# Dilated-window attention on one Trainium2 core: heads taken in pairs on halves of the TensorE array, groups combined in the same stage

## The chip, the core and the metric

The kernel runs on 1 core of one Trainium2 chip. The metric is the device time of one execution in microseconds (us). PE is TensorE (PEld its weight loads), DVE is VectorE, ACT is ScalarE, POOL is GpSimd and SP is the queue that issues every DMA here.

## The reference, cut to what matters

A sequence of 1024 prompt tokens and one of 256 sample tokens (1280 rows, 10 tiles of 128) go through an attention layer, a state-space layer and a last norm, all in float32. Only the attention layer is touched. It has three groups of 16 heads of 64 dims, with dilations 1, 4 and 16 and windows 128, 512 and 2048:

```python
proj = hn @ w_in                       # q, k, v of each group, and one gate z of 1024 columns
for g, (window, dilation) in enumerate(GROUP_PATTERNS):
    q = _rope(qkv[:, :, g, 0]); k = _rope(qkv[:, :, g, 1]); v = qkv[:, :, g, 2]
    o, lse = _dilated_window_attention(q, k, v, dilation, window // (2 * dilation))
wts = softmax(stack(lses), axis=0)     # per token and head, over the three groups
o = einsum('gbsh,gbshd->bshd', wts, stack(outs))
y = o.reshape(b, s, 1024) * silu(z)
return y @ w_out
```

## The kernel before, in words

Stages follow one another, each in its own block: `norm_stage`, `attend_stage`, `combine_stage`, `out_stage` ("mix"), two state-space stages ("front", "back"), "glu" and `out_stage` again ("final").

**Attend.** A unit is a pair of heads of one group, 24 units in all, group by group. `steps()` gives 25 rows: a row projects unit n while unit n-1 attends. A projection is three weight tiles (K, Q, V), each of three chunks of 512, 512 and 256 tokens, each chunk 8 k-tiles by 3 split products (`project`, L848; hi and lo parts in fp32r). A row has 22 slots; each slot gives PE one score (L794), one transpose step (L803), one value step (L816) of one head of one tile, and then 10 projection matmuls. The score of a head contracts 64 dims, so it uses 64 of PE's 128 rows: weights are 128 queries, up to 256 keys stream past. The key windows are 128, 192 or 256 wide (`windows`); the sample tiles of groups 1 and 2 use all 256 sample keys and a mask of residues. DVE adds the mask and takes the minimum (L721), ACT takes the exponential with its row sum (L642), PE transposes the probabilities, DVE copies them out (L731), and in the value step the transposed probabilities (128 keys by 128 queries) are the weights and 64 columns of values stream past, so the output is tokens by dims; ACT copies it out (L649) and SP stores it by token into `o_scratch`. The buffers `sc`, `sm`, `pr`, `tr`, `pt` have two halves, used by alternate steps.

Rope: SP swaps halves of K or Q by DMA (`sw`), POOL multiplies by the sine (L618), DVE by the cosine (L740) and adds (L752). At the start of a row the unit's V is transposed through `pj` (L828), and ACT copies it out before the next projection may use `pj`. POOL also computes 16 "powers" tasks for the state-space layer (64 or 65 steps, one task per row in rows 1 to 16), and stores each in DRAM.

**Combine.** The stage loads the gate weights, projects z (480 matmuls of 512 columns), loads the three groups' outputs and statistics, computes the group shares once for all heads, weighs and adds the three outputs, multiplies by silu(z), transposes y (80 transposes) and stores it to `y_scratch`. Beside that it loads the eight "f" results of POOL's tasks, transposes them (128 transposes) and stores them.

Every engine runs its instructions in the order written; waits are on semaphores.

Of the kernel before, what the change touches and what calls it, by code (L numbers as in the profile page):

```python
# [21 lines left out]
F32R = mybir.dt.float32r  # L22
# [4 lines left out]
P = 128  # L27
# [36 lines left out]
POWER_TASKS = 2 * NB  # L64
POWER_END = [L * 2 * (t + 1) + L * 6 * (t + 1) + max(t + 1 - NB, 0) for t in range(POWER_TASKS)]

MASKS = {"at0": (0, 256), "at64": (256, 256), "at128": (512, 256), "class64": (768, 128),
         "mod4": (896, 256), "mod16": (1152, 256)}  # L70
MASK_COLS = 1408


def mask_table(np):

    q = np.arange(P)[:, None]
    k = np.arange(256)[None, :]
    ok = [np.abs(k - q) <= HALF, np.abs(k - 64 - q) <= HALF, np.abs(k - 128 - q) <= HALF,
          (k[:, :128] // 64) == (q // 64), (k - q) % 4 == 0, (k - q) % 16 == 0]
    return np.where(np.concatenate(ok, axis=1), 0.0, -BIG).astype(np.float32)  # L80


def windows(g):
# [15 lines left out]
    first = len(value_blocks(g)) - 2  # L99
    for i in range(2):  # L100
        mask = ("at0", "at128")[i] if g == 0 else ("mod4" if g == 1 else "mod16")
        out.append((PROMPT, 256, mask, [(first, 128, 0), (first + 1, 128, 128)]))
# [284 lines left out]
ATT_STEPS = 2 * TILES  # L387
SLOTS = ATT_STEPS + 2
UNIT_MMS = 3 * len(CHUNKS) * KT
PER_SLOT = -(-3 * UNIT_MMS // SLOTS)  # L390
CHUNK_MMS = 3 * KT
K_TILE, Q_TILE, V_TILE = range(3)


def chunk_slot(c):

    return (CHUNK_MMS * (c + 1) - 1) // PER_SLOT


def attend_stage(nc, w_att, tables, masks_d, ident_d, hT, o_scratch, st_scratch, a, ab_d, decay_d,  # L400
                 seeds, placed_d):
    with ExitStack() as ctx:
        m = Mem(nc, ctx, "att")
        raw = m.sb("raw", [P, 2, KT, P])
        wh = m.sb("wh", [P, 3, KT, P], F32R)
        wl = m.sb("wl", [P, 3, KT, P], F32R)
# [4 lines left out]
        val = m.sb("val", [P, 2, 11, P])  # L411
# [4 lines left out]
        pt = m.sb("pt", [P, 2, 256])  # L416
        o_sb = m.sb("o", [P, TILES, P])
# [4 lines left out]
        place = m.sb("place", [P, 2, GB, L, SC])  # L422

# [4 lines left out]
        st = m.sb("stats", [P, TILES, HEADS, 2])  # L428
        pj = m.ps("pj", [P, 3, 512])
        sc = m.ps("sc", [P, 2, 512])  # L430
        tr = m.ps("tr", [P, 2, 512])
        po = m.ps("po", [P, 512])

# [8 lines left out]
        o_stored, seed_in, pool_step, place_stored = (  # L442
            m.sem(n) for n in ("o_stored", "seed_in", "pool_step", "place_stored"))
        st_stored = m.sem("st_stored")
# [3 lines left out]


        def steps():  # L450
            for n in range(UNITS + 1):
                yield (n - 1 if n >= 1 else None), (n if n < UNITS else None)

        def to_class_order(dst, src, g, lo, n):

            d = DILATION[g]
            if g == 0 or lo >= PROMPT:
                return dst[:, lo:lo + n], src[:, 0:n]
            a, b = lo // d, (lo + n) // d
            return (dst[:, 0:PROMPT].rearrange("p (r l) -> p r l", r=d)[:, :, a:b],  # L460
                    src[:, 0:n].rearrange("p (l r) -> p r l", r=d))

        @block.sync
        def _(sp):
            def raw_load(n):
                if n >= 2:
                    sp.wait_ge(w_hi, n - 1)
                    sp.wait_ge(w_lo, n - 1)
                sp.dma_start(raw[:, n % 2], w_att[n // 3, n % 3]).then_inc(raw_in[n % 2], 16)

            def swap(unit, which):
                n = 2 * unit + which
                sp.wait_ge(chunk_out, 9 * unit + 3 * (which + 1))
                if n >= 1:
                    sp.wait_ge(rope_done, n)
                for a in range(4):
                    b = a ^ 1
                    sp.dma_start(sw[32 * a:32 * a + 32, :], t[32 * b:32 * b + 32, which, :]).then_inc(swapped, 16)

            def by_class(sb, dram, g, done):  # L480

                if g == 1:
                    v = dram[0:PROMPT].rearrange("(a p r) c -> a p r c", a=2, r=4)
                    for a in range(2):
                        sp.dma_start(v[a], sb[:, a:PT:2, :]).then_inc(done, 16)
                elif g == 2:
                    v = dram[0:PROMPT].rearrange("(l i b) c -> b l i c", i=PT, b=2)
                    for b in range(2):
                        sp.dma_start(v[b], sb[64 * b:64 * b + 64, 0:PT, :]).then_inc(done, 16)
                else:  # L490
                    v = dram[0:PROMPT].rearrange("(h i p) c -> h p i c", h=2, p=P)
                    for h in range(2):
                        sp.dma_start(v[h], sb[:, 4 * h:4 * h + 4, :]).then_inc(done, 16)
                v = dram[PROMPT:TOK].rearrange("(i p) c -> p i c", p=P)
                sp.dma_start(v, sb[:, PT:TILES, :]).then_inc(done, 16)

            def load_seed(task):
                kind, b = divmod(task, NB)
                if task >= 1:
                    sp.wait_ge(pool_step, POWER_END[task - 1])  # L500
                    kind1, b1 = divmod(task - 1, NB)
                    sp.dma_start(seeds[kind1][:, :, b1 * GB:(b1 + 1) * GB], seed[:]).then_inc(place_stored, 16)
                    sp.dma_start(placed_d[kind1][b1], place[:].rearrange("p r g t c -> p r g (t c)"))\
                      .then_inc(place_stored, 16)
                if 1 <= task < POWER_TASKS:
                    sp.wait_ge(place_stored, 32 * task)
                if task < POWER_TASKS:
                    sp.dma_start(seed[:], a[("b", "c")[kind]][:, :, b * GB:(b + 1) * GB]).then_inc(seed_in, 16)

            def store(unit):  # L510
                g, pair = divmod(unit, PAIRS)
                sp.wait_ge(o_out, TILES * (unit + 1))
                by_class(o_sb[:], o_scratch[g][:, pair * P:(pair + 1) * P], g, o_stored)
                if pair == PAIRS - 1:
                    sp.wait_ge(expd, ATT_STEPS * (unit + 1))
                    by_class(st[:].rearrange("p i h s -> p i (h s)"), st_scratch[g], g, st_stored)
# [6 lines left out]
            raw_load(2)  # L523
            for j, name in ((4, "a_re"), (5, "a_im"), (6, "log_step")):
                sp.dma_start(params[:, j], a[name]).then_inc(param_in, 16)
            for att, proj in steps():
                if proj is not None and proj + 1 < UNITS:
                    raw_load(3 * (proj + 1) + K_TILE)
                if proj is None:
                    break  # L530
                if proj + 1 < UNITS:
                    raw_load(3 * (proj + 1) + Q_TILE)
                swap(proj, K_TILE)
                if proj + 1 < UNITS:
                    raw_load(3 * (proj + 1) + V_TILE)
# [7 lines left out]
                if 1 <= proj <= POWER_TASKS + 1:  # L543
                    load_seed(proj - 1)
# [1305 lines left out]
```

## Time and profile before

| | |
|---|---|
| runs | 2867.34, 2868.78, 2869.9 us (median 2868.78) |
| span of the profiled execution | 2864.4 us; its own time is not recorded, the span is 4.4 us below the median |
| PE / DVE / ACT / POOL busy over the span | 2581.1 / 1287.2 / 848.1 / 797.2 us |
| attend stage, from its first projection (us 53) | to us 1769 |
| combine stage | to us 1931 |
| later stages | us 1931 to 2864 |
| DMA | 298.43 MB, 33.4% of 16 engines' span |

Times in a profile are counted from the start of the span. A float32 matmul stands in the trace as two MATMUL records. A matmul's recorded duration includes its pipeline, so what it costs PE is read from the start of one record to the start of the next, not from the duration.

### The profile page before, as it was taken

The page shows a single profiled execution, that of the slowest core. Times are in us where ns is not written, and L with a number is a line of the kernel's source. Part 1 is how long each engine was busy: PE and PEld are TensorE (multiplying, and loading weights), DVE is VectorE, ACT ScalarE, POOL GpSimd, SP SyncE. Part 2 cuts the span into 40 slices and gives each one's busy share as a digit, 9 for nine tenths or more (in the row PEclk, how much of TensorE's full clock was granted, in tenths as well). Part 3 has the DMA queues.
Part 4 walks back from the last instruction along what each step waited for, and adds up shares of the span by engine and source line. Part 5 has one row for each costly group of instructions (what it writes and reads, how often), then busy time and mean ns, then how long its engine had stood idle before and what let it go on. Part 6 is the DMA issues. An engine that isn't in the chain of part 4 may idle for free. (4 is left out here: it accounts for less than half of the span.)

```text
span 2864.4 us, 39052 instructions
## 1 busy us (share of the span) xinstructions
PE 2581.1 (90%) x13832; PEld 2035.0 (71%) x13832; DVE 1287.2 (45%) x2871; ACT 848.1 (30%) x2178; POOL 797.2 (28%) x1303
## 2 busy tenths in 40 slices
PE   5999999999999999999999998898889993267978
PEld 4777777777777777777777776777678873265767
DVE  5333333334444444443344434754322799725434
ACT  4233233332223222223333333323244320014222
POOL 1644444444444444443101110211011110121200
PEclk9999999999999999999999996999999997588989
DMA  4122222222222222222212112876465450384333
GB/s 149 50 58 69 69 69 69 66 64 69 69 69 69 69 62 69 69 62 74 59 50 60 52 41 72 301 254 208 158 206 162 143 151 20 90 239 165 133 138 125
DMA packets 173481, 298.43 MB, mean 104 GB/s; under 512 B 32880, under 2 KB 107632, under 8 KB 170096
## 3 DMA queue, kind: packets, MB, share of 16 engines
q1 hardware_dynamic: 173296, 296.00, 33.4%
q8 instruction: 112, 1.84, 0.3%
q14 instruction: 73, 0.60, 0.1%
HBM read 177.80 MB, written 86.67 MB: 92 GB/s over the span
## 5 line engine op out<-in xcount | busy, mean ns | idle before, releaser
L848 PE MATMUL att_pj<-hT_hi,att_wh 128*128 128x512 f32 (+1 forms) x1728 | 633.7, 367 | 20.7 <-ACT att_val L674 10.6
L848 PE MATMUL att_pj<-hT_lo,att_wh 128*128 128x512 f32 (+1 forms) x1728 | 631.4, 365 | 0.0
L848 PE MATMUL att_pj<-hT_hi,att_wl 128*128 128x512 f32 (+1 forms) x1728 | 630.5, 365 | 0.0
L721 DVE CUSTOM_DVE_ANT_0 att_sm<-att_sc,att_mask 128x256 f32<-128x256 f32 (+2 forms) x480 | 179.9, 375 | 930.5 <-PE att_sc L794 915.6
L642 ACT ACTIVATE att_pr<-att_sm,att_stats 128x256 f32<-128x256 f32 (+2 forms) x480 | 225.7, 470 | 927.1 <-DVE att_stats L721 926.5
L618 POOL TENSOR_TENSOR att_sw<-att_sw,att_rope 128x1280 f32<-128x1280 f32 x48 | 146.2, 3045 | 913.8 <-DMA att_sw<-att_t 913.7
L848 PEld LDWEIGHTS att_pj<-hT_hi,att_wh 128*128 128x128 f32 x1728 | 328.1, 190 | 68.7 <-issue 17.6
L848 PEld LDWEIGHTS att_pj<-hT_hi,att_wl 128*128 128x128 f32 x1728 | 328.0, 190 | 43.6
L848 PEld LDWEIGHTS att_pj<-hT_lo,att_wh 128*128 128x128 f32 x1728 | 328.7, 190 | 41.5
L794 PE MATMUL att_sc<-att_qk 64*128 64x256 f32 (+2 forms) x960 | 302.9, 396 | 4.5 <-DVE att_qk L752 4.5
L816 PE MATMUL att_po<-att_val,att_pt 128*128 128x64 f32 (+1 forms) x1664 | 257.8, 266 | 0.0
L816 PEld LDWEIGHTS att_po<-att_val,att_pt 128*128 128x128 f32 (+1 forms) x1664 | 241.9, 198 | 9.5 <-issue 3.0
L794 PEld LDWEIGHTS att_sc<-att_qk 64*128 64x128 f32 x960 | 144.5, 189 | 141.1 <-issue 115.3
L803 PE MATMUL att_tr<-att_ident,att_pr 128*128 128x128 f32 (+1 forms) x832 | 197.7, 307 | 0.3 <-ACT att_pr L642 0.2
L803 PEld LDWEIGHTS att_tr<-att_ident,att_pr 128*128 128x128 f32 (+1 forms) x832 | 87.9, 138 | 120.4 <-issue 106.1
L667 ACT COPY att_t<-att_pj 128x512 f32<-128x512 f32 (+1 forms) x216 | 111.4, 516 | 200.0 <-PE att_pj L848 196.7
L731 DVE COPY att_pt<-att_tr 128x256 f32<-128x256 f32 (+1 forms) x384 | 145.7, 379 | 41.3 <-PE att_tr L803 39.8
L597 POOL TENSOR_TENSOR att_prod<-att_power,att_ab 128x128 f32<-128x128 f32 x416 | 158.0, 412 | 8.4
L158 PE MATMUL front_pj<-front_hh,front_wh 128*128 128x512 f32 (+1 forms) x384 | 139.9, 364 | 15.6 <-DVE front_hl L1445 15.6
L740 DVE TENSOR_TENSOR att_t<-att_t,att_rope 128x1280 f32<-128x1280 f32 x48 | 144.3, 3007 | 19.9 <-DMA att_sw<-att_t 19.8
L160 PE MATMUL front_pj<-front_hh,front_wl 128*128 128x512 f32 (+1 forms) x384 | 137.0, 357 | 0.0
L159 PE MATMUL front_pj<-front_hl,front_wh 128*128 128x512 f32 (+1 forms) x384 | 136.8, 356 | 0.0
(234 smaller groups left out, 3959.0 us busy)
## 6 DMA issues: line engine op xcount, KB each, us to landing
att_raw<-in_w_att_dram SPq DMA_DIRECT2D x72, 512.0 KB, 3.6
att_sw<-att_t SPq DMA_DIRECT2D x192, 160.0 KB, 2.8
comb_o<-o_scratch SPq DMA_DIRECT2D x60, 256.0 KB, 4.3
o_scratch<-att_o SPq DMA_DIRECT2D x48, 256.0 KB, 3.1
placed_f<-att_place SPq DMA_DIRECT2D x8, 1024.0 KB, 4.5
e_scratch<-att_place SPq DMA_DIRECT2D x8, 1024.0 KB, 4.5
comb_fpre<-placed_f SPq DMA_DIRECT2D x16, 512.0 KB, 5.5
f_scratch<-comb_ft SPq DMA_DIRECT2D x16, 512.0 KB, 4.0
```

The costliest lines, as they stand in the source:

```text
L158: pe.matmul(out, lh, rh, start=first, stop=False)
L160: return pe.matmul(out, ll, rh, start=False, stop=last)
L597: pool.tensor_tensor(prod[:, j], old[:, x], y, ALU.mult).then_inc(pool_step, 1)
L618: pool.tensor_tensor(sw[:], sw[:], rope[:, 1], ALU.mult).then_inc(sin_done, 1)
L642: act.activation(pr[:, n % 2, 0:w], sm[:, n % 2, 0:w], ACT.Exp, bias=st[:, s // 2, h, 0:1], scale=-1.0, accum_out=st[:, s // 2, h, 1:2]).t ...
L721: dve.tensor_tensor_reduce(sm[:, n % 2, 0:w], sc[:, n % 2, 0:w], mask[:, a:a + w], -SCALE, 3e38, ALU.add, ALU.min, st[:, s // 2, h, 0:1]). ...
L731: last = dve.tensor_copy(pt[:, n % 2, 0:P * len(pieces)], tr[:, n % 2, 0:P * len(pieces)])
L740: dve.tensor_tensor(t[:, which], t[:, which], rope[:, 0], ALU.mult).then_inc(cos_done, 1)
L794: pe.matmul(sc[:, n % 2, 0:w], qk[rows, unit % 2, Q_TILE, i * P:(i + 1) * P], qk[rows, unit % 2, K_TILE, k0:k0 + w], start=True, stop=True ...
L803: last = pe.transpose(tr[0:k, n % 2, j * P:(j + 1) * P], pr[:, n % 2, c0:c0 + k], ident[:])
L816: last = pe.matmul(po[:, h * HD:(h + 1) * HD], pt[0:k, n % 2, j * P:(j + 1) * P], val[0:k, unit % 2, b, h * HD:(h + 1) * HD], start=(j == ...
L848: last = pe.matmul(pj[:, c % 3, 0:n], w[:, which, kt], h[:, kt, lo:lo + n], start=(r == 0), stop=(r == CHUNK_MMS - 1))
```

## The change

`combine_stage` is gone. `attend_stage` now has units ordered pair by pair (the three groups of a pair one after another), 26 rows of 12 slots, and a fourth weight tile (Z) in every third unit. A slot handles one tile for both heads: two scores on rows 0 to 63 and 64 to 127 of PE into two banks, value steps whose weights are the values (64 columns for head 0, 64 for head 1) and whose moving operand is the transposed probabilities, so the output is dims by tokens with head 0 on partitions 0 to 63 and head 1 on 64 to 127, and then the transposes. Between slots come 18 projection matmuls (24 in rows with four weight tiles). Sample tiles of groups 1 and 2 are put into class order too, so that their windows are 128 wide. `sm`, `pr`, `pt`, `sc`, `tr` now have one half per head, and `val` one copy. The outputs stay on chip, in four buffers of 128 by 1280; ACT scatters classes back to tokens while copying. Per unit the statistics go to DRAM by token (SP: 1, 4 or 10 DMAs) and come back per pair (3 DMAs). In each row n = 4, 7, ... 25 DVE and ACT compute the shares of one pair, and in nine steps ACT spreads a share over 64 dims, PE transposes it into the bank `aux`, and DVE multiplies, adds and gates (18 instructions of up to 512 columns); SP stores y of the pair. The V transposes use `aux` as well, in three parts with projection matmuls between. POOL's 16 tasks lie in rows 2 to 17; the eight "f" results are transposed by PE in slots 3 to 6 of the row after (`f_turn`), copied by ACT and stored by SP, in place of the way over DRAM.

```diff
-        first = len(value_blocks(g)) - 2
-            mask = ("at0", "at128")[i] if g == 0 else ("mod4" if g == 1 else "mod16")
-            out.append((PROMPT, 256, mask, [(first, 128, 0), (first + 1, 128, 128)]))
+        if g == 0:
...
+        else:
+            out.append((P * i, 128, ("class64", "class16")[g - 1], [(i, 128, 0)]))
...
-SLOTS = ATT_STEPS + 2
-PER_SLOT = -(-3 * UNIT_MMS // SLOTS)
+SLOTS = STEPS + 2
+def per_slot(unit):
+    return 3 * w_count(unit) * CHUNK_MMS // SLOTS
...
             for n, att, proj, comb in rows():
                 if proj is not None:
                     raw_load(base + 2)
...
+                if n in TURN_ROW:
+                    f_store(TURN_ROW[n], 0)
+                if proj is not None:
+                    raw_load(base + 3)
+                    swap(proj, K_TILE)
...
+                    stats_store(att)
+                    if att % GROUPS == GROUPS - 1:
+                        stats_load(att // GROUPS)
...
+            def combine(pair, k):
...
+                dve.wait_ge(bcast_done, 9 * pair + k + 1)
+                dve.tensor_tensor(own, own, aux[:, 0:n], ALU.mult).then_inc(comb_step, 1)
+                if g >= 1:
+                    dve.wait_ge(comb_step, at + 1)
+                    dve.tensor_tensor(own, own, before, ALU.add).then_inc(comb_step, 1)
+                if g == 2:
+                    dve.wait_ge(comb_step, at + 2)
+                    dve.tensor_tensor(own, own, gate[:, cols], ALU.mult).then_inc(comb_step, 1)
...
             def score(unit, s):
-                n = ATT_STEPS * unit + s
-                if n >= 2:
-                    pe.wait_ge(masked, n - 1)
-                rows = slice(64 * h, 64 * h + 64)
-                pe.matmul(sc[:, n % 2, 0:w], qk[rows, unit % 2, Q_TILE, i * P:(i + 1) * P],
-                          qk[rows, unit % 2, K_TILE, k0:k0 + w], start=True, stop=True).then_inc(scored, 1)
+                n = STEPS * unit + s
+                if n >= 1:
+                    pe.wait_ge(masked, 2 * n)
+                for h in range(2):
+                    head = slice(64 * h, 64 * h + 64)
+                    pe.matmul(sc[:, h, 0:w], qk[head, unit % 2, Q_TILE, s * P:(s + 1) * P],
+                              qk[head, unit % 2, K_TILE, k0:k0 + w], start=True, stop=True).then_inc(scored, 1)
...
             def values(unit, s):
...
                 for j, (b, k, _) in enumerate(pieces):
-                    last = pe.matmul(po[:, h * HD:(h + 1) * HD], pt[0:k, n % 2, j * P:(j + 1) * P],
-                                     val[0:k, unit % 2, b, h * HD:(h + 1) * HD],
-                                     start=(j == 0), stop=(j == len(pieces) - 1))
+                    for h in range(2):
+                        head = slice(64 * h, 64 * h + 64)
+                        last = pe.matmul(po[head, 0:P], val[0:k, b, head], pt[0:k, h, j],
+                                         start=(j == 0), stop=(j == len(pieces) - 1))
...
+            def f_turn(task, q, att):
+                if q == 0:
+                    pe.wait_ge(pool_step, POWER_END[task])
+                    pe.wait_ge(vturn_out, 3 * (att + 1))
...
+                for j in range(4):
+                    last = pe.transpose(aux[:, j * P:(j + 1) * P],
+                                        place[:, j % 2, 2 * q + j // 2].rearrange("p t c -> p (t c)"), ident[:])
...
                     if att is not None and s < STEPS:
                         score(att, s)
+                    if att is not None and s >= 2:
+                        values(att, s - 2)
+                    if att is not None and 1 <= s <= STEPS:
                         turn(att, s - 1)
...
+                    if n in TURN_ROW and 3 <= s < 7:
+                        f_turn(TURN_ROW[n], s - 3, att)
+                    if comb is not None and s >= 3:
+                        broadcast(comb, s - 3, att)
...
-def combine_stage(nc, w_z, ident_d, hT, o_scratch, st_scratch, y_scratch, placed_f, f_scratch):
```

## Rows read from the trace of the kernel before

**Rows 1.** Stretches: us, busy PE PEld DVE ACT POOL (records), PEclk, DMA share, GB/s.

```profile
103.00:1737.00 1634.00, 1619.34 (x8553) 1229.79 (x8553) 649.38 (x1670) 496.91 (x1509) 622.30 (x1150) 1.00 0.22 63
1737.00:1769.00 32.00, 31.68 (x120) 23.29 (x118) 12.48 (x58) 13.16 (x52) 0.00 (x0) 0.58 0.09 21
1769.00:1931.00 162.00, 138.60 (x689) 115.91 (x688) 99.17 (x132) 49.66 (x91) 29.97 (x20) 0.92 0.81 268
```

**Rows 2.** PE in order of time, 256-wide step: start us, us, line, matmul, count.

```profile
634.97 0.28 PE L848 MATMUL att_pj<-hT_hi,att_wh 128*128 128x256 f32 x1
635.08 0.28 PE L848 MATMUL att_pj<-hT_lo,att_wh 128*128 128x256 f32 x1
635.29 0.70 PE L794 MATMUL att_sc<-att_qk 64*128 64x256 f32 x2
635.92 0.44 PE L803 MATMUL att_tr<-att_ident,att_pr 128*128 128x128 f32 x2
636.20 0.56 PE L816 MATMUL att_po<-att_val,att_pt 128*128 128x64 f32 x4
636.56 0.36 PE L848 MATMUL att_pj<-hT_hi,att_wl 128*128 128x256 f32 x1
636.76 0.28 PE L848 MATMUL att_pj<-hT_hi,att_wh 128*128 128x256 f32 x1
```

**Rows 3.** The same of a 128-wide step, with two 512-column projections ahead.

```profile
1384.66 0.40 PE L848 MATMUL att_pj<-hT_hi,att_wl 128*128 128x512 f32 x1
1384.89 0.40 PE L848 MATMUL att_pj<-hT_hi,att_wh 128*128 128x512 f32 x1
1385.22 0.48 PE L794 MATMUL att_sc<-att_qk 64*128 64x128 f32 x2
1385.63 0.33 PE L803 MATMUL att_tr<-att_ident,att_pr 128*128 128x128 f32 x1
1385.80 0.33 PE L816 MATMUL att_po<-att_val,att_pt 128*128 128x64 f32 x2
1385.94 0.47 PE L848 MATMUL att_pj<-hT_lo,att_wh 128*128 128x512 f32 x1
1386.25 0.39 PE L848 MATMUL att_pj<-hT_hi,att_wl 128*128 128x512 f32 x1
```

**Rows 4.** PE in the front stage: matmuls on rows 0-63 (L1509) and 64-127 (L1513).

```profile
2252.03 0.27 PE L1509 MATMUL front_states_ps<-front_f,front_ub 64*16 64x112 f32 x1
2252.04 0.27 PE L1513 MATMUL front_states_ps<-front_f,front_ub 64*16 64x112 f32 x1
2252.13 0.26 PE L1509 MATMUL front_states_ps<-front_f,front_ub 64*16 64x112 f32 x1
```

**Rows 5.** POOL in order of time: the Q sine, and the end of the task after it.

```profile
825.77 2.91 POOL L618 TENSOR_TENSOR att_sw<-att_sw,att_rope 128x1280 f32<-128x1280 f32 x1 [21.48 <-DMA att_sw<-att_t]
...
862.61 0.85 POOL L570 COPY att_place<-att_power 64x256 f32<-64x256 f32 x2
```

**Rows 6.** Groups by line and form, us 103 to 1737: busy us, mean ns, idle before.

```profile
L740 DVE TENSOR_TENSOR att_t<-att_t,att_rope 128x1280 f32<-128x1280 f32 x46 | 141.4, 3073 | 0.6 <-DMA att_sw<-att_t 0.5
L721 DVE CUSTOM_DVE_ANT_0 att_sm<-att_sc,att_mask 128x256 f32<-128x256 f32 x252 | 106.5, 422 | 417.0 <-PE att_sc L794 416.4
L642 ACT ACTIVATE att_pr<-att_sm,att_stats 128x256 f32<-128x256 f32 x252 | 128.4, 510 | 533.7 <-DVE att_stats L721 533.4
```

**Rows 7.** The last row, PE in order of time, two scores one step apart.

```profile
1754.65 0.79 PE L794 MATMUL att_sc<-att_qk 64*128 64x128 f32 x2
...
1756.11 0.79 PE L794 MATMUL att_sc<-att_qk 64*128 64x128 f32 x2
```

**Rows 8.** A DVE group of the combine stage, us 1769 to 1931.

```profile
L1028 DVE TENSOR_TENSOR comb_o<-comb_o 128x512 f32<-128x512 f32 x20 | 13.8, 692 | 0.7
```

**Rows 9.** DMA issues of one line on SP: ns min/median/max, first and last start.

```profile
L495 SPq DMA_DIRECT2D st_scratch<-att_stats x3: 556/624/639, 691.4 to 1773.7; - x3
```

**Rows 10.** DMA issues: count, KB each, median us from issue to landing.

```profile
comb_stats<-st_scratch SPq DMA_DIRECT2D x3, 160.0 KB, 4.3
```

More of the change, by code:

```diff
@@ L510, in store @@
[L510 to L516, printed above, removed]
+                for x in range(4):
+                    y = x ^ 1
+                    sp.dma_start(sw[32 * x:32 * x + 32, :], t[32 * y:32 * y + 32, which, :]).then_inc(swapped, 16)
@@ new lines, in f_evac, with share_exp @@
+            def f_evac(task, q):
+                b = POWERS[task][2]
+                act.wait_ge(f_turned, 4 * b + q + 1)
+                if 4 * b + q:
+                    act.wait_ge(f_stored, 16 * (4 * b + q))
+                if q == 0 and POWERS[task][0] >= 4:
+                    act.wait_ge(bcast_done, 9 * ((POWERS[task][0] - 1) // GROUPS))
+                act.copy(ft[:], aux[:].rearrange("p (g r n) -> p g r n", g=2, r=2)).then_inc(f_out, 1)
+            def share_exp(pair):
+                act.wait_ge(shares, SHARE_STEPS * pair + 3)
+                act.activation(ex[:], gap[:], ACT.Exp).then_inc(exps, 1)
@@ new lines, in share_spread @@
+            def share_spread(pair, k):
+                g, c = divmod(k, 3)
+                lo, n = CHUNKS[c]
+                i, tiles = lo // P, n // P
+                if k == 0:
+                    act.wait_ge(shares, SHARE_STEPS * (pair + 1))
+                    act.wait_ge(f_stored, 16 * 4 * sum(1 for row in TURN_ROW if row < GROUPS * pair + 4))
+                else:
+                    act.wait_ge(bcast_done, 9 * pair + k)
+                act.copy(wide[:, 0:2 * tiles].rearrange("p (i h) d -> p i h d", h=2),
+                         share[:, i:i + tiles, g].unsqueeze(3).to_broadcast([P, tiles, 2, HD])).then_inc(spread, 1)
@@ L742, in rotate @@
             def rotate(unit, which):
-                n, g = 2 * unit + which, unit // PAIRS
+                n, g = 2 * unit + which, unit % GROUPS
                 dve.wait_ge(cos_done, n + 1)
@@ new lines, in value_turn @@
+            def value_turn(unit, b):
+                blocks = value_blocks(unit % GROUPS)
+                if unit + b:
+                    pe.wait_ge(vturn_out, 3 * unit + b)
+                if b == 0:
+                    pe.wait_ge(const_in, 48)
+                    pe.wait_ge(chunk_out, 3 * (w_base(unit) + 3))
+                    turns = sum(1 for row in TURN_ROW if row <= unit)
+                    if turns:
+                        pe.wait_ge(f_out, 4 * turns)
+                    if unit >= 4:
+                        pe.wait_ge(comb_step, COMB_STEPS * ((unit - 1) // GROUPS))
+                for j in range(4 * b, min(4 * b + 4, len(blocks))):
+                    k0, k = blocks[j]
+                    last = pe.transpose(aux[0:k, (j - 4 * b) * P:(j - 4 * b + 1) * P], t[:, 0, k0:k0 + k], ident[:])
+                last.then_inc(vturn_done, 1)
@@ new lines, in broadcast @@
+            def broadcast(pair, k, att):
+                g, c = divmod(k, 3)
+                lo, n = CHUNKS[c]
+                pe.wait_ge(spread, 9 * pair + k + 1)
+                if k == 0:
+                    pe.wait_ge(vturn_out, 3 * (UNITS if att is None else att + 1))
+                else:
+                    pe.wait_ge(comb_step, COMB_STEPS * pair + comb_steps(k - 1) + 1)
+                for j in range(n // P):
+                    last = pe.transpose(aux[:, j * P:(j + 1) * P],
+                                        wide[:, 2 * j:2 * j + 2].rearrange("p h d -> p (h d)"), ident[:])
+                last.then_inc(bcast_done, 1)
```

791 lines of the change are left out of this document (358 added, 433 removed).

## The prediction

> **What bounds the kernel now.** I cut the span into stretches first. From us 103 to 1737, the 23 rows in which one unit projects while another attends, PE is busy 1619 of 1634 us at the full clock of 2.4 GHz, while DVE has 649, ACT 497 and POOL 622 [rows 1]. So a row lasts as long as PE's own list, 71.0 us each, and only work taken from that list, or a new wait in it, changes the time. Then come 32 us for the last unit, with nothing to project and a granted clock of 0.58, mostly the lower level of 1.2 GHz, and 162 us of combine, in which PE is busy 139 us, mostly with z [rows 1].
>
> Second I read PE in order of time around one step, from start to start. A 512-column projection record takes 0.23 us (1384.66 to 1384.89), a 256-column one about 0.12 (636.76 less its 0.08 of delay, below). The 256-wide step of one head takes: 0.09 from the end of the projection (635.08 + 0.12) to the score, 0.63 for the score's two records, 0.28 for two transposes, 0.36 for the values' four records, 0.08 by which the second projection behind it is late: 1.44 us [rows 2]. The 128-wide step takes 0.10, 0.41, 0.17, 0.14 and 0.08: 0.90 us [rows 3]. The differences give unit prices. 128 more columns in each of two score records cost 0.22 us, so 0.11 us per 128 columns and record. One transpose costs 0.11 (0.28 less 0.17), with 0.06 fixed. Two value records cost 0.22, 0.11 each, though only 64 columns stream, half of what 0.11 us carries: there the 128-column weight load sets the pace. Of a 128-wide score's 0.41, 0.22 stream; 0.19 are a first weight load (0.11) and the change of array shape (0.08). Third, the front stage has two chains of float32 matmuls on rows 0 to 63 and 64 to 127: 112 columns in steps of 0.10 us (2252.03 to 2252.13), the other half 0.01 behind [rows 4]. Halves by rows run side by side.
>
> **The change, part by part.** *Scores.* Both heads side by side cost one head's score plus 0.11 for the second half's weights: 0.74 for 256 keys, 0.52 for 128. *Values.* The weights are now 64 columns (0.055, an estimate: half the load above), 128 columns stream (0.11 a record), two records per head and piece. No row shows halves by columns. Bounds: wholly side by side, 0.11 x 4 for a wide tile; one after the other, 0.11 x 8. I take side by side, since the nearest row, the halves by rows, is [rows 4]. With two first loads (0.11) and a change of shape (0.09) that is 0.64, narrow 0.42. *Transposes* stay 0.11 each: 0.06 + 0.44, narrow 0.06 + 0.22. A wide tile of both heads so costs 0.09 + 0.74 + 0.64 + 0.50 + 0.08 = 2.05 in place of 2.88; a narrow one 1.40 in place of 1.80; a sample tile of groups 1 and 2, wide before and narrow now, 1.40 in place of 2.88.
>
> The Trainium skill, "TensorEngine Tiling (Array Packing)", Key Properties, has tiles of columns, too, load and multiply in parallel; by that the sum stays as it is, and no run here shows it yet.
>
> In the 23 rows stand 8 units each of groups 0 and 1 and 7 of group 2: 80 + 64 wide tiles (0.83 saved), 30 sample tiles (1.48), 56 narrow ones (0.40): 119.5 + 44.4 + 22.4 = 186 us off PE. Two smaller ends of the list I take by estimate: the tiles with a 64-key piece change shape once more per head before and once per pair now (48 tiles, some 0.4 us each from the 0.09 and 0.11 above: 19 us), and PE no longer waits for the V copies before it projects (some 0.4 us a row, an ACT copy: 10 us). The rows then take 1634 - 186 - 29 = 1419 us.
>
> *Added to PE.* z moves in with the same columns, 480 x 0.23 = 110 us. The f transposes: 128 x 0.11 + 32 x 0.1 = 17. The shares: 30 transposes and nine changes a pair, 30 x 0.11 + 9 x 0.15 = 4.7, seven pairs: 33. Rows 1 to 23: 1579 us. A single row: projection 144 x 0.23 + 72 x 0.12 = 42 us (56 with a Z tile), its ten tiles 20.5, 19.2 or 14.0 for groups 0, 1, 2, V and the rest 1 to 2, shares 4.7 in rows that attend group 0: about 69, 78 and 58 us.
>
> *Covered work.* DVE gains 18 instructions a pair at 0.69 [rows 8] or less, some 11 us; with its 28 us a row (649 over 23) and statistics it holds some 45 us in a row of 69. ACT and DVE per tile: two masks at 0.42 and two exponentials at 0.51, each with a short read of its sum [rows 6]: 2.5 us in line, while the transposes wait for the exponentials only one slot later. Slots are 4.8 to 6.5 us long (those rows by 12). The cosine, 3.07 us [rows 6], stands ahead of the next mask on DVE; two such slots per row can shift a mask by a microsecond or three, inside that slack. `o_scratch` and the f detour were DMA beside PE in the rows (DMA share 0.22 [rows 1]): nothing. The per-unit statistics are 1, 4 or 10 issues at 0.62 us [rows 9] on SP behind the row's loads; the shares read them a slot and a half into the next row, some 15 us on: nothing, and if that cover is gone, DVE and ACT stop in slot 1 and PE at the score of slot 3. SP's f stores stand ahead of the K load and swap; they delay a swap by some 3 us in four rows, and the rotation has more than a slot.
>
> *The new wait.* `f_turn` puts PE behind POOL. From a Q sine's start to its task's end POOL takes 37.7 us (825.77 to 863.46) [rows 5]. In a 69 us row the sine starts at about 8 slots + 4.5 us = 50.5, the task ends at 88, `f_turn` comes at 69 + 3 x 6.5 + 1.5 = 90: 2 us to spare, four times; 9 us the other four times. Behind `f_turn` are queued the slot's 18 or 24 projections and the next score. I put 10 us for all waits, 0 to 40 as bounds.
>
> *The end.* Before, 194 us follow the last full row [rows 1]. Now: ten slots of the last unit at the low clock (a step of one head takes 1.46 there [rows 7], a pair some 2.2): 24 with the V transposes; then in line ten issues of statistics at 0.62 and their landing (2.3, an estimate at half of the 4.3 of a load [rows 10]), three loads and 4.3 [rows 9, 10]: 14.7; shares 3; nine steps of transposes, multiply, add, gate at 0.69 [rows 8]: 16; the store of y 3.5. 61 us, bounds 50 to 75.
>
> **Sum.** 1579 + 10 + 61 = 1650 in place of 1634 + 194 = 1828: 178 us less. The span of 2864.4 becomes 2686; the median lies 4.4 us above the span, so 2691, rounded to **2690 us**. 0.2% (6 us) is about what a measurement of this kernel tells from no change.
>
> **Rivals.**
> *Columns in turn.* The two column halves stream one after the other: 144 x 0.44 + 86 x 0.22 = 82 us more: 2772. For it: no row shows the contrary; against it: halves by rows. Chance 0.13.
> *Loads in turn, too.* Every value record waits for its own 64-column load, as both halves share the same rows: 8 x 0.055 a wide tile and 4 x 0.055 a narrow one more, 82 us again: 2854. Against it: the old value records, all on the same rows, start 0.11 apart [rows 2, 3], the time of the load alone; load and stream in turn would be 0.165. Chance 0.03. The Trainium skill, "TensorE: Matmul & The Clock Gate", Part 3, says that a weight load overlaps matmuls in flight only when the row group differs; by that this rival would be the time, and the trace disagrees.
> *POOL holds PE: slower.* Place: `f_turn` in slot 3 of eight rows. A busier DVE or a late swap lengthens the task; each us past the 2 (or 9) to spare is a us of PE. It decides from some 28 us of added length in each of eight tasks (178 / 8 = 22, and the slack of 5 or 6): with tasks longer by 31 us, about twice theirs, 2690 + 4 x 29 + 4 x 22 = 2894. Against it: POOL took the same steps beside a DVE at 40% [rows 1, 5]. Chance 0.04.
> *No overlap at all.* Rows and columns both in turn (scores dearer by 0.32 and 0.11: 56 us): 2690 + 82 + 56 = 2828. Against it stand rows 4. Chance 0.02.
>
> **Numbers.** The forecast has 0.78. Its own range: 32 us lower if the second loads (0.14 a tile, 230 tiles) hide as well, 10 without waits, 11 with a short end: 2637; 30 us higher with the waits at their bound: 2720, and 14 for the end. Taking in the first rival with some waits, 2635 to 2785. Faster 0.95, within 0.2% 0.01, slower 0.04.
>
> **What would show it.** Right: attention rows of about 69, 78 and 58 us with PE over 97% busy; in one slot score to values 0.74 and to the transposes 0.64 more; value records of head 1 beginning within 0.06 of head 0's. Wrong: value records all 0.11 or 0.16 apart in one line; PE idle at `f_turn` with POOL as releaser; DVE or ACT waiting for the statistics; an end much longer than 61 us.

## The result, and the profile after

The changed kernel takes **2628.35 us** (median of 4 runs, 2625.17 to 2635.17) in place of 2868.34 (2867.34 to 2869.9, 4 runs): a ratio of 0.9168, 95% interval 0.9154 to 0.9181. The forecast was 2690, its range 2635 to 2785: the time lies 62 us under the forecast and 7 under the low end. The profiled execution took 2628.88 us, its span is 2627.0.

The same cut into stretches as [rows 1]: rows 1 to 23, then the end of the attend stage (last unit, last shares, store of y), then mix and all behind it.

```profile
101.00:1632.00 1531.00, 1507.71 (x9287) 1187.43 (x9287) 639.82 (x1583) 578.71 (x1667) 693.55 (x1141) 1.00 0.24 64
1632.00:1697.00 65.00, 30.39 (x135) 16.83 (x133) 21.41 (x76) 21.59 (x66) 0.00 (x0) 0.52 0.08 12
1697.00:2627.00 930.00, 722.99 (x4176) 608.29 (x4176) 477.72 (x909) 249.39 (x459) 115.53 (x77) 0.89 0.47 150
```

PE still sets the rows: busy 1508 of 1531 us, at a granted clock that rounds to 1.00 (three short stretches at the lower level stand below). By the starts of the V transposes, rows 1 to 23 last from 100.9 to 1631.6, 1530.7 us, where 1589 was forecast (1579 and 10 of waits). The end lasts to 1697.4: 65.8 us, forecast 61, bounds 50 to 75. So the miss lies in the rows, 58 us.

One wide tile of both heads, PE in order of time, beside [rows 2]:

```profile
1200.15 0.39 PE L1066 MATMUL att_pj<-hT_hi,att_wl 128*128 128x512 f32 x1
1200.47 0.70 PE L982 MATMUL att_sc<-att_qk 64*128 64x256 f32 x4
1201.10 0.66 PE L1005 MATMUL att_po<-att_pt,att_val 128*64 128x128 f32 x8
1201.69 0.66 PE L992 MATMUL att_tr<-att_ident,att_pr 128*128 128x128 f32 x4
1202.10 0.36 PE L1066 MATMUL att_pj<-hT_hi,att_wh 128*128 128x256 f32 x1
1202.30 0.28 PE L1066 MATMUL att_pj<-hT_lo,att_wh 128*128 128x256 f32 x1
...
1258.18 0.28 PE L1066 MATMUL att_pj<-hT_hi,att_wl 128*128 128x256 f32 x1
1258.39 0.49 PE L982 MATMUL att_sc<-att_qk 64*128 64x128 f32 x4
1258.81 0.44 PE L1005 MATMUL att_po<-att_pt,att_val 128*64 128x128 f32 x4
1259.18 0.44 PE L992 MATMUL att_tr<-att_ident,att_pr 128*128 128x128 f32 x2
1259.37 0.36 PE L1066 MATMUL att_pj<-hT_hi,att_wh 128*128 128x256 f32 x1
1259.57 0.28 PE L1066 MATMUL att_pj<-hT_lo,att_wh 128*128 128x256 f32 x1
```

Read from start to start. The four score records of both heads take 0.63 us to the values, exactly what the two records of one head took in [rows 2]. Eight value records take 0.59, though eight in line would stream for 0.88. Four transposes take 0.41. With 0.09 ahead (1200.15 + 0.23 to 1200.47) and 0.08 behind (1202.30 - 1202.10, less 0.12) the tile costs 1.80 us; the forecast was 2.05. The narrow tile, below it, costs 0.09 + 0.42 + 0.37 + 0.19 + 0.08 = 1.15 in place of 1.40.

PE's waits within the rows (releaser: us in total, times, longest):

```profile
PE att_aux L1024 <- ACT att_val L782: 12.4, 15, 1.1
PE att_aux L1035 <- POOL att_place L653: 9.5, 4, 2.6
```

L1024 are the V transposes, L1035 the f transposes: the "new wait" of the prediction is there, four times. Of the 12.4 us at V, 12.1 fall in the seven rows that attend group 2.

### The profile page after: what moved, and what is told of

Same layout as the page of the kernel before. It is cut to its first block and busy times, and to the rows that moved or that the text cites. A ratio compares the mean times of both kernels' runs of the same rounds, so it can differ in the third digit from the quotient of the medians.

```text
span 2627.0 us, 38336 instructions
## 1 busy us (share of the span) xinstructions
PE 2325.1 (89%) x13896; PEld 1865.8 (71%) x13896; DVE 1185.6 (45%) x2668; ACT 886.2 (34%) x2256; POOL 841.2 (32%) x1283
## 5 line engine op out<-in xcount | busy, mean ns | idle before, releaser
L1066 PE MATMUL att_pj<-hT_hi,att_wh 128*128 128x512 f32 (+1 forms) x1920 | 710.0, 370 | 10.8 <-DVE att_wl L848 10.8
L860 DVE CUSTOM_DVE_ANT_0 att_sm<-att_sc,att_mask 128x128 f32<-128x128 f32 (+2 forms) x480 | 152.4, 355 | 561.6 <-PE att_sc L982 560.4
L730 ACT ACTIVATE att_pr<-att_sm,att_stats 128x128 f32<-128x128 f32 (+2 forms) x480 | 215.0, 449 | 434.1 <-PE att_tr L992 313.0
L879 DVE TENSOR_TENSOR att_t<-att_t,att_rope 128x1280 f32<-128x1280 f32 x48 | 71.8, 1495 | 201.8 <-DMA att_sw<-att_t 201.8
L870 DVE COPY att_pt<-att_tr 128x512 f32<-128x512 f32 (+1 forms) x192 | 107.0, 557 | 110.2 <-PE att_tr L992 110.0
L1005 PE MATMUL att_po<-att_pt,att_val 128*64 128x128 f32 (+1 forms) x1536 | 146.5, 295 | 6.4 <-ACT att_o L751 5.9
L982 PE MATMUL att_sc<-att_qk 64*128 64x128 f32 (+2 forms) x960 | 146.0, 382 | 0.0
L992 PE MATMUL att_tr<-att_ident,att_pr 128*128 128x128 f32 (+1 forms) x768 | 138.8, 294 | 0.0
L1005 PEld LDWEIGHTS att_po<-att_pt,att_val 128*64 128x64 f32 (+1 forms) x1536 | 79.0, 136 | 72.8 <-issue 52.9
L891 DVE TENSOR_TENSOR att_qk<-att_t,att_sw 128x1024 f32<-128x1024 f32 (+1 forms) x80 | 107.9, 1383 | 48.4 <-issue 34.9
```

The lines of the kernel that those rows point to most:

```text
L730: act.activation(pr[:, h, 0:w], sm[:, h, 0:w], ACT.Exp, bias=st[:, unit % 2, s, h, 0:1], scale=-1.0, accum_out=st[:, unit % 2, s, h, 1:2]) ...
L860: dve.tensor_tensor_reduce(sm[:, h, 0:w], sc[:, h, 0:w], mask[:, x:x + w], -SCALE, 3e38, ALU.add, ALU.min, st[:, unit % 2, s, h, 0:1]).the ...
L982: pe.matmul(sc[:, h, 0:w], qk[head, unit % 2, Q_TILE, s * P:(s + 1) * P], qk[head, unit % 2, K_TILE, k0:k0 + w], start=True, stop=True).th ...
L992: last = pe.transpose(tr[0:k, h, j], pr[:, h, c0:c0 + k], ident[:])
L1005: last = pe.matmul(po[head, 0:P], val[0:k, b, head], pt[0:k, h, j], start=(j == 0), stop=(j == len(pieces) - 1))
L1066: last = pe.matmul(pj[:, c % 3, 0:n], w[:, k % 2, kt], h[:, kt, lo:lo + n], start=(r == 0), stop=(r == CHUNK_MMS - 1))
```

## Experiments on the halves

The theory after this reading: the second half, of rows or of columns, costs PE nothing at all, neither its stream nor its weight load. Rival 1 is the prediction's own price (the second load is paid, 0.11 us for scores and 0.055 for values), with the 58 us coming from elsewhere; rival 2 is halves in turn.

**One head's scores left out.**

```diff
-                for h in range(2):
-                    head = slice(64 * h, 64 * h + 64)
-                    pe.matmul(sc[:, h, 0:w], qk[head, ...], qk[head, ...]).then_inc(scored, 1)
+                pe.matmul(sc[:, 0, 0:w], qk[0:64, ...], qk[0:64, ...]).then_inc(scored, 2)
```

> Left out: the score of head 1 (its mask step reads head 0's scores instead), so PE issues half of the score matmuls. Theory (the row half of head 1 loads its weights and streams wholly beside head 0): nothing is saved, 2628 us within 5. Rival 1 (the second half's weight load is paid in turn, 0.11 us a tile, as the prediction had it, and the 58 us by which rows 1 to 23 are shorter came from elsewhere): 240 tiles x 0.11 = 26 us less, 2602. Rival 2 (row halves stream in turn): 144 wide tiles x 0.44 + 96 narrow x 0.22 = 84 us less, 2544.

**One head's values left out.**

```diff
-                    for h in range(2):
-                        last = pe.matmul(po[head, 0:P], val[0:k, b, head], pt[0:k, h, j], ...)
+                    last = pe.matmul(po[0:64, 0:P], val[0:k, b, 0:64], pt[0:k, 0, j], ...)
```

> Left out: the value matmuls of head 1 (its half of the output stays zero), so PE issues half of the value matmuls. Theory (the column half of head 1 loads and streams wholly beside head 0): nothing is saved, 2628 us within 5. Rival 1 (second half's load paid in turn, 0.055 us a tile by the prediction's estimate): 240 x 0.055 = 13 us less, 2615. Rival 2 (column halves in turn): 144 x 0.44 + 96 x 0.22 = 84 us less, 2544.

**Both heads through the columns of one, and both through the rows of one.**

```diff
-                        last = pe.matmul(po[head, 0:P], val[0:k, b, head], pt[0:k, h, j], ...)
+                        last = pe.matmul(po[0:64, 0:P], val[0:k, b, head], pt[0:k, h, j], ...)
```

> Changed: head 1's values go through the column half of head 0 (both heads are added into partitions 0 to 63), the same number of matmuls with the same sizes. Theory (the change lives from two column halves working at once): each record of head 1 costs its 0.11 us of streaming, 144 x 4 x 0.11 + 96 x 2 x 0.11 = 84 us more, 2712; with its load of 0.055 in turn as well 126 us more, 2754. Rival 2 (column halves work in turn already): no difference, 2628 within 5.

```diff
-                    head = slice(64 * h, 64 * h + 64)
+                    head = slice(0, 64)
                     pe.matmul(sc[:, h, 0:w], qk[head, ...], qk[head, ...])
```

> Changed: head 1's score reads the queries and keys of head 0, on rows 0 to 63, the same number of matmuls with the same sizes. Theory (two row halves at once): 144 x 0.44 + 96 x 0.22 = 84 us more, 2712, and up to 26 us more where the second load of 0.11 us is not hidden: 2738. Rival 2 (row halves in turn already): no difference, 2628 within 5.

**Half of the transposes left out**, for a price to compare with.

```diff
-                for h in range(2):
-                    for j, (_, k, c0) in enumerate(pieces):
-                        last = pe.transpose(tr[0:k, h, j], pr[:, h, c0:c0 + k], ident[:])
+                for j, (_, k, c0) in enumerate(pieces):
+                    last = pe.transpose(tr[0:k, 0, j], pr[:, 0, c0:c0 + k], ident[:])
```

> Left out: the transposes of head 1's probabilities (head 0's are copied into both places), so PE issues half of the transposes. If each transpose costs 0.11 us of PE, as 16 f transposes cost 1.77 in a row of f_turn_later: rows that attend group 0 shorter by 2 x 10 x 0.11 = 2.1 to 2.2 us, group 1 by 2.0, group 2 by 1.1; in all 144 x 0.22 + 96 x 0.11 = 42 us, less some 8 that the four rows that wait for POOL keep: about 34 us less than the changed kernel, 2595. If transposes hide beside other work as the second halves do: rows the same and 2628 to 2631.

Medians: 2632.14 and 2630.15 us with half of the scores or of the values gone, 2690.05 and 2699.0 with both heads on one half of the rows or columns, 2599.41 with half of the transposes; the changed kernel itself, run again beside others, 2630.93. In rows without f transposes (from one row's first V transpose to the next; us):

| kernel | attends group 0, with shares | group 1, with a Z tile | group 2, with the waits at V |
|---|---|---|---|
| changed kernel | 64.53 | 73.57 | 57.07 |
| half the scores | 64.48 | 73.49 | 57.01 |
| half the values | 64.47 | 73.50 | 57.01 |
| scores on one row half | 68.52 | 76.96 | 59.00 |
| values on one column half | 68.88 | 77.42 | 59.22 |
| half the transposes | 62.39 | 71.69 | 55.95 |

Half of the matmuls of a step can go and a row of ten tiles gets 0.05 to 0.08 us shorter: rival 1 wanted 1.1 for the scores, 0.55 for the values. Put on one half, the same matmuls cost 0.40 us per wide score (64.53 to 68.52 in ten tiles) and 0.43 per wide value step: rival 2 falls by its own price. One wide tile of each, PE in order of time; first half the values, then values on one column half, then scores on one row half:

```profile
1184.56 0.70 PE L984 MATMUL att_sc<-att_qk 64*128 64x256 f32 x4
1185.19 0.65 PE L1007 MATMUL att_po<-att_pt,att_val 128*64 128x128 f32 x4
1185.77 0.66 PE L994 MATMUL att_tr<-att_ident,att_pr 128*128 128x128 f32 x4
```

```profile
1187.85 0.70 PE L984 MATMUL att_sc<-att_qk 64*128 64x256 f32 x4
1188.48 1.09 PE L1010 MATMUL att_po<-att_pt,att_val 128*64 128x128 f32 x8
1189.50 0.66 PE L994 MATMUL att_tr<-att_ident,att_pr 128*128 128x128 f32 x4
```

```profile
1181.57 1.13 PE L982 MATMUL att_sc<-att_qk 64*128 64x256 f32 x4
1182.63 0.66 PE L1005 MATMUL att_po<-att_pt,att_val 128*64 128x128 f32 x8
1183.21 0.66 PE L992 MATMUL att_tr<-att_ident,att_pr 128*128 128x128 f32 x4
```

Values take 0.58 us for four records on one half and 0.59 for eight on two; 1.02 for eight on one. Scores take 1.06 on one half and 0.63 on two. The transposes do cost: 2.14 us for twenty in a row of group 0, 0.11 each. Both kernels with heads on one half came out at 60 to 70 us more, not 84. Part of that is 0.40 and 0.43 in place of 0.44 a tile; the rest lies in the four rows of group 1 with f transposes. There the longer list took the place of the wait for POOL: PE waits for it 0.3 us once with values on one column half, and the profile lists no such wait with scores on one row half, so these rows stayed near the changed kernel's 77.9 to 79.8 (78.7 to 79.8 us). Half the transposes came out at 30 less, not 34: the same rows stayed at 78.7 to 80.2, since the four waits for POOL grew to 3.4 to 3.8 us each.

**The sample tiles.** Undone alone:

```diff
-            out.append((P * i, 128, ("class64", "class16")[g - 1], [(i, 128, 0)]))
+            out.append((PROMPT, 256, ("mod4", "mod16")[g - 1], [(PT, 128, 0), (PT + 1, 128, 128)]))
...
-ST_DMAS = (1, 4, 10)
+ST_DMAS = (1, 3, 3)
...
```

> Undone: the narrow sample tiles of groups 1 and 2 (their windows are all 256 sample keys again, with masks of residues; to make room the exponentials of the gaps are made in place). By the measured prices of a wide and a narrow tile (1.80 and 1.15) each such tile costs 0.65 more: rows that attend groups 1 and 2 longer by 1.3 us; rows 1 to 23: 30 x 0.65 = 20 less about 5 that the four rows waiting for POOL take up; the end: two tiles dearer by some 1 us and seven issues of statistics fewer, 7 x 0.63 = 4.4 us less. In all 10 to 13 us more than the changed kernel, 2640. Rival (the rows have slack there, or the scattered copies and ten issues cost as much as they save): within 4 us of it.

2657.13 us (2651.52 to 2659.64), 26 more than the changed kernel, where 10 to 13 were expected. Rows that attend groups 1 and 2 take 74.85 and 58.35, 1.28 more for two tiles: 0.64 a tile, as the two tiles above say (1.80 - 1.15), and 20 us over the rows. Two parts of the expectation fell. The four rows that wait for POOL took nothing up: the task they wait for begins in a row that attends group 0, which this edit leaves as it was. And the end stayed at 66 us with seven issues fewer: the last unit's V transposes and slots took 0.9 us more, as expected of two dearer tiles, and the statistics only 1.0 less. SP's DMA issues at the end, first of the changed kernel, then of this one:

```profile
1661.40 1.19 SPq L549 DMA_DIRECT2D st_scratch<-att_stats  x2
1662.63 5.07 SPq L554 DMA_DIRECT2D st_scratch<-att_stats  x8
1668.88 1.88 SPq L561 DMA_DIRECT2D att_pair_stats<-st_scratch  x3
```

```profile
1683.92 1.20 SPq L548 DMA_DIRECT2D st_scratch<-att_stats  x2
1685.16 1.48 SPq L549 DMA_DIRECT2D st_scratch<-att_stats  x1
1690.43 1.79 SPq L556 DMA_DIRECT2D att_pair_stats<-st_scratch  x3
```

From the first store to the load are 7.5 us with ten issues and 6.5 with three. SP waits 3.8 us behind the last of three issues and 1.2 behind the last of ten, since it is the one large store that is late: it holds both sample tiles and lands 5.3 us after its issue begins, while the last of the eight small pieces (an eighth of the sample rows each) lands 1.7 us after its own. The span of this profile is 21 us above that of the changed kernel run again (2649.7 and 2628.7), the median 26; the profiled execution was the fastest of the four, and the other 5 us stand in no profile.

## Experiments on the waits

**The f transposes one slot later**, with their copies; SP issues the stores behind the K swap.

```diff
-                    if n in TURN_ROW and 3 <= s < 7:
-                        f_turn(TURN_ROW[n], s - 3, att)
+                    if n in TURN_ROW and 4 <= s < 8:
+                        f_turn(TURN_ROW[n], s - 4, att)
```

> Edit: the f transposes, their copies and stores one slot later (slots 4 to 7). Theory (the 9.5 us that PE idles there in 4 pieces, with POOL as releaser, are the end of POOL's task, 2.3 to 2.6 us late against a slot of 6.5): 9.5 us less, about 2619, and no wait for POOL left. Rival (the stores then hold up the swap of Q or the next loads on SP, and the wait moves to the scores of the next row): no gain, 2628 or up to 10 us more.

**Silu one row later**, where no exponentials follow in the row.

```diff
-                        if s == SLOTS - 1 and w_count(proj) == 4:
-                            silu(proj)
+                    if att is not None and s == STEPS and w_count(att) == 4:
+                        silu(att)
...
                 act.activation(gate[:], gate[:], ACT.Silu).then_inc(gated, 1)
+                act.activation(warm[:], ident[0:1, 0:1], ACT.Exp)
```

> Edit: silu of the gate goes from the last slot of the row that projects z to slot 10 of the next row, where no exponentials are left, and a one-element exponential behind it brings the table of exponentials back there. Theory (the V transposes at the start of a row behind z wait for ACT, which then has two table loads of 1.28 us and a silu of 1.27 in hand): about 2.5 us less in each of 7 rows and 2 to 4 us less in the last row: 16 to 20 us less, about 2610. Rival (the waits of the V transposes, 16.4 us in 17 pieces, are those for ACT's copies alone, in any row): no more than 4 us less.

> The changed kernel as it is, beside the next three: 2628 us, rows 1 to 23 within 2 us of 1531.

> Both edits together. If they are independent: 25 to 30 us less than the changed kernel, 2598 to 2603; if both only fill the same slack of PE, no better than the better of the two.

Together on one chip: changed kernel 2630.93 us, f transposes later 2618.03, silu later 2623.78, both 2608.1 (again, on another occasion, 2610.54). The ratios to before are 0.9175 (0.9163 to 0.9188), 0.9125 (0.9113 to 0.9138), 0.9151 (0.9139 to 0.9164) and 0.9093 (0.9081 to 0.9106). The gains alone, 12.9 and 7.2 us, add up to 20.1, and both together gave 22.8: the edits are independent, though below the 25 to 30 expected, since silu gave too little. The rows of the changed kernel took 1527.7 us in this second profile, not within 2 of 1531; the reason is the clock, next.

The f transposes gave 12.9 us, more than the 9.5 of idle time, and no wait of PE for POOL is left. The rows that waited fell to 75.33 each: from 79.31, 79.79, 79.45 and 77.89 in the first profile of the changed kernel, 15.1 us, and from 79.47, 78.21, 77.89 and 77.89 in the second, 12.1 us. Why more than the idle time, PE in order of time shows in the first profile:

```profile
381.92 1.12 PE L1035 MATMUL att_aux<-att_ident,att_place 128*128 128x128 f32 x4 [2.30 <-POOL att_place L653]
382.69 0.78 PE L1066 MATMUL att_pj<-hT_hi,att_wh 128*128 128x512 f32 x1
383.27 0.63 PE L1066 MATMUL att_pj<-hT_lo,att_wh 128*128 128x512 f32 x1
383.69 0.63 PE L1066 MATMUL att_pj<-hT_hi,att_wl 128*128 128x512 f32 x1
384.12 0.63 PE L1066 MATMUL att_pj<-hT_hi,att_wh 128*128 128x512 f32 x1
384.55 0.59 PE L1066 MATMUL att_pj<-hT_lo,att_wh 128*128 128x512 f32 x1
384.97 0.40 PE L1066 MATMUL att_pj<-hT_hi,att_wl 128*128 128x512 f32 x1
385.21 0.40 PE L1066 MATMUL att_pj<-hT_hi,att_wh 128*128 128x512 f32 x1
```

Behind 2.30 us of idle the 512-column records start 0.43 us apart until 384.97 and 0.24 after: the lower level of the clock (1.2 GHz) until then, the higher (2.4 GHz) after. The granted clock over 4 us from the first f transpose on is 0.62 here, 0.69 and 0.57 behind the second and third wait, and 1.00 behind the fourth (us 990.57), also of 2.30 us, whose row is the one of 77.89. So with the same idle time the lower clock cost 1.4 us (79.31 less 77.89). In the second profile the same four waits are there, 2.3 to 2.6 us, but the clock fell behind the first alone (0.61, then 1.00 three times): that is why its rows are 3 us shorter.

Silu gave less than expected: 7.2 us in the medians. In the profiles each of the seven rows that attend group 2 is 0.8 us shorter (58.06 for 58.87, 56.28 for 57.07), 5.6 in all, and the end 5.1 (60.7); that profiled execution, 2618.69 us, was the fastest of five. ACT in order of time, end of a row of that kernel; ACT_TABLE_LOAD stands ahead of silu and, again, ahead of the exponential:

```profile
1482.27 0.59 ACT L773 COPY att_t<-att_pj 128x512 f32<-128x512 f32 x1 [2.71 <-PE att_pj L1069]
1482.87 1.28 ACT L777 ACT_TABLE_LOAD   x1
1484.16 1.27 ACT L777 ACTIVATE att_gate<-att_gate 128x1280 f32<-128x1280 f32 x1
1485.45 1.28 ACT L778 ACT_TABLE_LOAD   x1
1486.75 0.20 ACT L778 ACTIVATE att_warm<-att_ident 1x1 f32<-1x1 f32 x1
1486.86 0.34 ACT L752 COPY att_o<-att_po 128x128 f32<-128x128 f32 x1
1487.02 0.40 ACT L773 COPY att_t<-att_pj 128x256 f32<-128x256 f32 x1
```

The copy at 1487.02 is that of V's last chunk, for which the V transposes of the next row wait; PE starts them at 1487.62 after 1.45 us of idle. The wait had only moved a row. ACT idled 2.71 us ahead of all this, so the mend is to put silu there:

```diff
                     if att is not None and s >= 2:
                         o_evac(att, s - 2)
...
+                    if att is not None and s == STEPS and w_count(att) == 4:
+                        silu(att)
...
-                    if att is not None and s == STEPS and w_count(att) == 4:
-                        silu(att)
```

That edit stands on top of one for the end, which came first:

```diff
-                sp.wait_ge(expd, 2 * STEPS * (unit + 1))
+                final = unit == UNITS - 1
+                sp.wait_ge(expd, 2 * (STEPS * unit + (PT if final else STEPS)))
...
+                if final:
+                    sp.wait_ge(expd, 2 * STEPS * UNITS)
-                for x in range(classes):
+                for x in range(classes // 2 if final else classes):
...
+                    if att == UNITS - 1 and s == STEPS:
+                        act.wait_ge(expd, 2 * STEPS * UNITS)
...
+                        for x in range(4, 8):
+                            act.dma_start(v[x], st[16 * x:16 * x + 16, ...]).then_inc(st_stored, 16)
```

> Edit on top of both_later, for the last unit alone: the two prompt pieces of its statistics are stored before its sample tiles are done, and four of the eight sample pieces are issued by ACT beside SP's four. If the end is in line with SP's issues (0.62 us each, ten of them): two plus four fewer in line, 3.7 us less, 2604. If the landing of the last store or ACT sets it: no difference, 2608.

> Both later edits as they are, beside the kernel before: 2608 us within 3.

> Edit on top of stats_split: in slot 10 silu and the one-element exponential stand ahead of the copy of the V chunk, where ACT idled 2.7 us, and no longer behind it. In silu_later the wait of 1.45 us came back at the start of the next row: there the V transposes wait for the copy of the last V chunk, for which ACT is late by two table loads and silu. Theory (all waits of the V transposes are ACT's table loads and silu in its order): 6 rows x 1.45 = 8.7 us less than stats_split, about 2595, and no wait of over 0.7 us left at the V transposes. Rival (the wait is for ACT's copies themselves): rows as in stats_split, 2604.

With the statistics split 2604.04 us (2598.67 to 2607.05), beside 2610.54 without. The end, from the last unit's V transposes to the start of mix, shrank from 62.0 to 59.5: 2.5 of the 3.7. SP's issues end sooner, but ACT begins its four at us 1639.34, 1.1 behind SP's second lot, and the load (1643.11) waits for the last of them, begun at 1641.31 and landed 1.8 us later. SP's issues there:

```profile
1632.84 1.19 SPq L551 DMA_DIRECT2D st_scratch<-att_stats  x2
1638.22 2.68 SPq L558 DMA_DIRECT2D st_scratch<-att_stats  x4
1643.11 1.74 SPq L565 DMA_DIRECT2D att_pair_stats<-st_scratch  x3
```

With silu ahead of the copy, **2598.06 us** (2597.02 to 2599.03), ratio to before 0.9061 (0.9049 to 0.9073): faster than both kernels of this case, 1.2% below the changed one. Rows 1 to 23 are 9.3 us shorter than with the statistics split alone (8.7 expected); a row that attends group 2 takes 54.92. The wait that had moved a row stands in the profiles mostly without a releaser ("issue"). Two lines show it with both later edits (the statistics split has the same 8.7 and 1.5 us), the third line what is left of it with silu ahead of the copy; then comes the stretch of that kernel's rows:

```profile
PE att_aux L1030 <- issue: 8.7, 6, 1.5
PE att_aux L1030 <- ACT att_t L776: 1.5, 1, 1.5
PE att_aux L1039 <- issue: 0.2, 1, 0.2
```

```profile
101.00:1601.00 1500.00, 1498.15 (x9281) 1184.40 (x9280) 630.76 (x1580) 578.81 (x1673) 682.99 (x1140) 1.00 0.24 65
```

PE is now busy 1498 of 1500 us; of its waits at the V transposes one of 0.3 us for ACT's copies is the longest left in the rows, where the changed kernel had 12.4 in all. So the waits at the V transposes were silu and its two table loads in ACT's order, not the copies.

## Why the prediction was right, and where it failed

**Right.** The mechanism and the sign: the rows are PE's list, and the pair on two halves shortens it. The values on two column halves were the choice made without a row, and it held. Covered work stayed covered: no wait of PE within the rows names DVE or a DMA. Rivals *columns in turn*, *loads in turn, too* and *no overlap at all* fall by the runs with one half, where the values cost 0.43 more a wide tile, the scores 0.40. The Trainium skill, "TensorEngine Tiling (Array Packing)", Key Properties, has separate tiles load weights and multiply in parallel; the trace agrees, with eight value records in 0.59 us. "TensorE: Matmul & The Clock Gate", Part 3, of the Trainium skill, lets a weight load overlap matmuls in flight only where the row group differs; the two column halves use the same 128 rows and the trace disagrees: half of their loads and streams left out saves 0.06 us in a row of ten wide tiles (64.53 to 64.47).

**The step that failed** is the size of the tile's terms, "2.05 in place of 2.88; a narrow one 1.40". Each is 0.25 us too dear, on 230 tiles 57.5 us, which is the miss; plain rows last 64.5, 73.6 and 57.1 us where 69, 78 and 58 were forecast (the last holds some 2 us for ACT's silu: 54.92 with silu moved). Of the 0.25, 0.11 are "plus 0.11 for the second half's weights" in the scores: both heads take 0.63, one head's time, and dropping one saves nothing. 0.05 lie in the values, 0.59 for 0.64 ("two first loads"). 0.09 lie in the transposes, "0.06 + 0.44": the projection starts 0.41 after the first of four and 0.19 after the first of two, 0.10 a transpose and nothing fixed. The 0.06 had been read where a value step followed the transposes, and now a projection follows, whose delay of 0.08 is counted by itself; that this is why the 0.06 is gone was not tested. The text had priced hidden second loads as "32 us lower" inside its own range, at 0.14 a tile (they are 0.16), but not the transposes; with both it would have reached 2633.

**Terms that were off and cancelled.** Shares: 2.8 us a pair (64.53 with them, 61.72 in the one row that attends group 0 without), not 4.7: 13 us less in seven pairs. Thirty transposes at 0.11 would be 3.3, so the nine changes of 0.15 that were added to them do not show; no run left the shares out. f transposes: 1.77 us a row (75.33 less 73.56), 14 in all, not 17: 16 transposes at 0.11, without the changes of 0.1. Waits: 12.4 at V, 9.5 for POOL and 5.6 behind it, most of it low clock, 27.5 in place of 10; in the second profile the last is 2.6. Together -57.5 - 13 - 3 + 17.5 = -56, and measured are -58.

**POOL holds PE.** The place and the mechanism were right, the slack was not: "2 us to spare, four times" became 2.3 to 2.6 us too late. `f_turn` was due, in the first of the four, 84.6 us after the start of the row before, not 90, mostly since that row is 64.5 long and not 69; the task ended at 86.8, not 88. It took 38.5 us from the Q sine's start, not 37.7, with a Q sine that is 1.3 us longer than in [rows 5] (below). Its price, a us of PE for a us of lateness, was too low as well, since the clock can fall behind the idle time. It stayed far from the 28 us per task from which it would have decided.

**The end.** 65.8 for 61, within bounds: V transposes and slots took 29.8 (1631.6 to 1661.4) and not 24; statistics, shares and the nine steps 31.7 (to 1693.1) and not 33.7; the store of y 4.2, for 3.5 that no row had given. Issues plus landing came to 7.5 us up to the load, where 6.2 + 2.3 were forecast: behind ten issues 1.2 us of landing are left.

## What to carry to other kernels

Where two float32 matmuls use separate halves of the array, by rows or by columns, price the pair at the time of one, weight loads included (shown here for 128 and 256 columns past halves of 64 rows, and 128 columns past halves of 64 columns), and read a step from start to start, so that what runs beside the next step isn't counted twice. When an engine's order moves a wait, look at the first instruction behind the moved one that somebody else waits for: silu had to stand in an idle gap, not merely in another row. A wait of 2.30 us on PE cost 2.56 us of the row where the clock stayed and 3.98 where it fell behind it (77.89 and 79.31 less 75.33), and one profile doesn't tell how often it falls.

## What was not expected of the hardware

The clock: behind three of four waits of 2.3 to 2.6 us PE ran its next records at 1.2 GHz, 0.43 us apart, which cost 1.4 us in the case shown. It isn't tied to a place: in the same kernel profiled again the clock fell behind one of the four, and in the six profiles that have four such waits each (2.3 to 2.8 us: both of the changed kernel, half the scores, half the values, wide sample tiles, silu later) the granted clock fell behind 15 of 24. What decides it was not found.

Cosine and sine changed places. Both multiply 1280 columns and wait for the same swap. In [rows 6] the cosine on DVE took 3.07 us, and the sine on POOL 2.91 in [rows 5]; in the changed kernel's page (busy us, mean ns, idle before) they are:

```profile
L704 POOL TENSOR_TENSOR att_sw<-att_sw,att_rope 128x1280 f32<-128x1280 f32 x48 | 201.5, 4198 | 762.9 <-DMA att_sw<-att_t 762.8
L879 DVE TENSOR_TENSOR att_t<-att_t,att_rope 128x1280 f32<-128x1280 f32 x48 | 71.8, 1495 | 201.8 <-DMA att_sw<-att_t 201.8
```

The cosine takes half of its time, the sine 1.3 us more. What sets who is slowed was not tried.
